# First layer of a four-layer trunk: 24 modulation chunks loaded in eleven groups, and their products placed elsewhere around the eight attention tiles

## The reference, cut to what matters

```python
def ada_mod(cond, w, b):
    m = jax.nn.silu(cond) @ w + b
    return [a[:, None, :] for a in jnp.split(m, 6, axis=-1)]
...
        sh1, sc1, gt1, sh2, sc2, gt2 = ada_mod(c, w_ada[li], b_ada[li])
        zsh1, zsc1, zgt1, zsh2, zsc2, zgt2 = ada_mod(cz, w_ada[li], b_ada[li])
        hx = modulate(x, norm_g[li, 0], sh1, sc1)
        hz = modulate(z, norm_g[li, 0], zsh1, zsc1)
        ...
            ox, oz = diff_attention(hx, hz, da_w_qkv[ia], da_w_o[ia], da_lambda[ia], da_subln[ia],
                                    lam_init, rows, cols, need_ctx)
        ...
        x = x + gt1 * ox
        x = x + gt2 * swiglu(modulate(x, norm_g[li, 1], sh2, sc2), ffn_in[li], ffn_out[li])
```

## Time and profile before

| what | value |
|---|---|
| median of 3 runs | 2442.58 us (2442.09, 2442.58, 2444.91) |
| time of the profiled execution | 2447.18 us |
| span of the profiled execution | 2445.4 us |
| PE busy | 2405.9 us (98%), 12338 matmuls |
| PE weight loads busy | 1983.0 us (81%) |
| VectorE busy | 1316.7 us (54%) |
| ScalarE busy | 1001.8 us (41%) |
| GpSimd busy | 1107.1 us (45%) |
| DMA | 340.62 MB, mean 139 GB/s |

### The profile page before, as it was taken

The page is one execution under the profiler, slowest core; times in us unless marked ns, Lnnn a source line. Parts: engine busy times, 40 slices in busy tenths (PEclk is TensorE's granted clock), DMA queues, the critical chain, the costliest instruction groups (busy, mean ns, idle before and its releaser), DMA issues.

```text
span 2445.4 us, 37489 instructions
## 1 busy us (share of the span) xinstructions
PE 2405.9 (98%) x12338; PEld 1983.0 (81%) x12338; DVE 1316.7 (54%) x2347; ACT 1001.8 (41%) x2023; POOL 1107.1 (45%) x839
## 2 busy tenths in 40 slices
PE   9999999999999999999999999999999999999998
PEld 4566788888888888888888887778888888778998
DVE  8997876647253334346664243655766524475321
ACT  3565442232243434433323234664323324466553
POOL 0432444445444344435445434223544543435896
PEclk9999999999999999999999999999999999999999
DMA  8362445556232222235555324222565532323654
GB/s 343 114 112 102 134 159 206 195 173 224 87 100 86 73 73 86 86 104 206 197 182 193 116 79 113 80 84 95 206 206 195 183 111 80 101 78 116 185 181 129
DMA packets 120869, 340.62 MB, mean 139 GB/s; under 512 B 35537, under 2 KB 41937, under 8 KB 120145
## 3 DMA queue, kind: packets, MB, share of 16 engines
q1 hardware_dynamic: 112754, 333.97, 41.8%
q10 hardware_dynamic: 8032, 5.52, 1.6%
HBM read 334.76 MB, written 4.69 MB: 139 GB/s over the span
## 4 chain that ended last, share of the span: by engine, by line
PE 50%; issue 31%; POOL 12%; DVE 4%; ACT 2%; DMA 1%; POOLq 0%; DVEq 0%; ACTq 0%; SPq 0%
PE low_banks L627 39%; POOL w_lo L620 12%; PE high_banks L627 10%; DVE h_lo L1964 1%; DVE tmp L1945 1%; DVE ssum_rstd L1801 0%; ACT w_hi L1276 0%; ACT e_x L1439 0%; DMA xT<-in_xT 0%; DVE rot L2139 0%; DMA ada_raw<-in_ada_w 0%; ACT lnm L1300 0%; DVE ssum_rstd L1933 0%; POOLq L619 0%; DMA w_raw<-in_weights 0%
## 5 line engine op out<-in xcount | busy, mean ns | idle before, releaser
L620 POOL TENSOR_TENSOR w_lo<-w_raw,w_hi 128x512 fp32r<-128x512 f32 x832 | 1106.7, 1357 | 1319.3 <-ACT w_hi L1276 1318.6
L627 PE MATMUL low_banks<-h_hi,w_hi 128*128 128x512 f32 (+2 forms) x1792 | 639.4, 357 | 5.0 <-POOL w_lo L620 1.8
L1276 ACT ACTIVATE w_hi<-w_raw 128x512 fp32r<-128x512 f32 x832 | 473.9, 624 | 395.4 <-PE low_banks L627 192.4
L627 PE MATMUL low_banks<-h_lo,w_hi 128*128 128x512 f32 (+2 forms) x1792 | 632.2, 353 | 0.0
L627 PE MATMUL low_banks<-h_hi,w_lo 128*128 128x512 f32 (+2 forms) x1792 | 630.6, 353 | 0.0
L1801 DVE SCALAR_TENSOR_TENSOR ssum_rstd<-ada_raw,high_banks 128x1024 f32<-128x1024 f32 x304 | 370.7, 1220 | 42.8 <-DMA ada_raw<-in_ada_w 33.9
L627 PEld LDWEIGHTS low_banks<-h_hi,w_hi 128*128 128x128 f32 x1792 | 337.9, 189 | 60.9 <-issue 4.8
L627 PEld LDWEIGHTS low_banks<-h_lo,w_hi 128*128 128x128 f32 x1792 | 338.1, 189 | 46.3 <-issue 1.0
L627 PEld LDWEIGHTS low_banks<-h_hi,w_lo 128*128 128x128 f32 x1792 | 337.1, 189 | 46.6
L1709 ACT ACTIVATE lnm<-low_banks 128x512 f32<-128x512 f32 x66 | 39.4, 597 | 378.2 <-PE low_banks L627 378.2
L2462 DVE TENSOR_TENSOR tmp<-low_banks,lnm 128x512 f32<-128x512 f32 x66 | 45.6, 692 | 211.3 <-ACT lnm L1709 207.6
(11 more groups left out here) (279 smaller groups left out, 3803.6 us busy)
## 6 DMA issues: line engine op xcount, KB each, us to landing
w_raw<-in_weights SPq DMA_DIRECT2D x424, 512.0 KB, 3.7
ada_raw<-in_ada_w SPq DMA_DIRECT2D x152, 512.0 KB, 3.8
ada_first<-in_ada_w SPq DMA_DIRECT2D x24, 512.0 KB, 9.1
v_all<-in_ada_w SPq DMA_DIRECT2D x10, 512.0 KB, 5.5
bias<-rpb_skew SPq DMA_DIRECT2D x64, 64.0 KB, 2.4
rpb_skew<-rpb_rows ACTq DMA_DIRECT2D x1, 3556.0 KB, 34.0
ada_rest<-in_ada_w SPq DMA_DIRECT2D x6, 512.0 KB, 14.0
cond_l<-in_cond SPq DMA_DIRECT2D x3, 1024.0 KB
```

What stands on the lines that cost most here:

```text
L620: nc.gpsimd.tensor_tensor(out=w_lo[:, r, part], in0=w_raw[:, r, part], in1=w_hi[:, r, part], op=ALU.subtract).then_inc(lo_ready, 1)
L627: return nc.tensor.matmul(dst, lhsT, rhs, start=start, stop=stop, **kw)
L1276: nc.scalar.activation(w_hi[:, r, part], w_raw[:, r, part], ACT.Copy).then_inc(hi_ready, 1)
```

## The change

It changes the tables, the place of the loads in SyncE's stream, and which chunks share one bias addition. The number of products (48) and of loads (24) stays.

```diff
-ADA_GROUPS = ((16, 0, (16, 17, 0, 4, 1, 5)), (22, 1, (2, 6, 3, 7)), (26, 0, (3,)), (27, 1, (7, 20, 21)),
-              (30, 0, (3, 7)), (32, 1, (20, 21, 22)), (35, 0, (20, 23)), (37, 1, (21, 22)), (39, 0, (20,)))
+ADA_GROUPS = ((16, 0, (16, 17, 0, 1, 5, 2)), (22, 1, (6, 3)), (24, 0, (7, 20)), (26, 1, (21, 3)), (28, 0, (7, 20)),
+              (30, 1, (21, 3)), (32, 0, (22, 20)), (34, 1, (21,)), (35, 0, (22, 23)), (37, 1, (20, 21)), (39, 0, (22,)))
 ADA_MIXER = 40
-ADA_VALUES = 4
-ADA_TILE = ((0, 1, 2), (1, 1, 1), (1, 1, 2), (1, 1, 2), (1, 1, 2), (1, 1, 2), (1, 1, 2), (1, 1, 2))
-ADA_TAIL = (1, 9)
+ADA_VALUES = 3
+ADA_TILE = ((0, 1, 1), (0, 0, 2), (1, 3, 0), (1, 3, 0), (1, 3, 0), (1, 3, 0), (1, 3, 1), (1, 3, 1))
+ADA_TAIL = (1, 10)
...
-            load_range(at, 24)
-
-            sp.wait_ge(ada_done, 25)
+            load_range(at, 22)
+
+            sp.wait_ge(plan[0].vst_ready, 2)
+            sp.wait_ge(ada_done, 22)
             ada_rest_load(2)
+            load_range(22, 24)
+
+            sp.wait_ge(plan[0].vst_ready, 4)
+            sp.wait_ge(ada_done, 24)
+            ada_rest_load(3)
+
+            sp.wait_ge(ada_done, 26)
+            ada_rest_load(4)
             load_range(24, 26)
...
+            sp.wait_ge(ada_done, 32)
+            ada_rest_load(7)
             load_range(30, plan[0].nf)
             at = plan[0].nf
 
-            sp.wait_ge(ada_done, 33)
             sp.wait_ge(plan[0].vst_ready, KT)
-            ada_rest_load(6)
+            sp.wait_ge(ada_done, 34)
+            ada_rest_load(8)
 
             sp.wait_ge(ada_done, 35)
-            ada_rest_load(7)
-
-            sp.wait_ge(ada_done, 36)
-            ada_rest_load(8)
+            ada_rest_load(9)
+
+            sp.wait_ge(ada_done, 37)
+            ada_rest_load(10)
...
-                    row = (a - a0) % LOOPED
+                    row = (a - ADA_FIRST) % LOOPED
...
-                        if row == LOOPED - 1 or a == a0 + len(slots) - 1:
-                            ada_sums(a - row, a - row, row + 1)
+                        if row == LOOPED - 1:
+                            ada_sums(a - row, a - row, LOOPED)
```

More of the change, by code:

```diff
@@ L511, in _ @@
             at = KT + RING
-            load_range(at, 24)
-            sp.wait_ge(ada_done, 25)
+            load_range(at, 22)
+            sp.wait_ge(plan[0].vst_ready, 2)
+            sp.wait_ge(ada_done, 22)
             ada_rest_load(2)
+            load_range(22, 24)
[4 more added lines that the diff above has]
+            ada_rest_load(4)
             load_range(24, 26)
-            sp.wait_ge(ada_done, 26)
-            sp.wait_ge(plan[0].vst_ready, 4)
-            ada_rest_load(3)
+            sp.wait_ge(ada_done, 28)
+            ada_rest_load(5)
             load_range(26, 28)
-            sp.wait_ge(ada_done, 28)
-            ada_rest_load(4)
+            sp.wait_ge(plan[0].vst_ready, 6)
+            sp.wait_ge(ada_done, 30)
+            ada_rest_load(6)
             load_range(28, 30)
-            sp.wait_ge(ada_done, 30)
-            sp.wait_ge(plan[0].vst_ready, 6)
-            ada_rest_load(5)
+            sp.wait_ge(ada_done, 32)
+            ada_rest_load(7)
             load_range(30, plan[0].nf)
             at = plan[0].nf
-            sp.wait_ge(ada_done, 33)
             sp.wait_ge(plan[0].vst_ready, KT)
-            ada_rest_load(6)
+            sp.wait_ge(ada_done, 34)
+            ada_rest_load(8)
             sp.wait_ge(ada_done, 35)
-            ada_rest_load(7)
-            sp.wait_ge(ada_done, 36)
-            ada_rest_load(8)
+            ada_rest_load(9)
+            sp.wait_ge(ada_done, 37)
+            ada_rest_load(10)
             def bias_load(L, t, slot, reused):
```

## The result

The changed kernel takes 2446.12 us (median of 22 runs, 2444.13 to 2450.25), the kernel before 2442.95 us (22 runs, 2440.93 to 2446.72). The ratio is 1.0014, with a 95% interval of 1.0008 to 1.002: some 3 us slower, and within the 0.2% that was called no difference. The forecast was 2444.9 us, which was 2.3 us over the median of three runs that stood before it (2442.58) and is 1.2 us under the measured one.

The account below looks back on a forecast made before the run. PE, busy 98% of the span, was taken to bound the kernel. Tile 7's scores 4.0 us earlier, 1.7 back in tail and projection: 2447.18 - 2.3 = 2444.9 us, range 2438.5 to 2451.5.

Parts of the forecast that it names:

- What bounds the kernel: Whole kernel: PE busy 98% of the span, so only its gaps and its clock can give time back.
- The fall in the other runs: Kernel before: the median run has the load wait but not the profiled execution's clock fall of 4.85 us.
- Up to T1: Until tile 1's scores start: fewer products ahead, gain 4.6 us, start at 108.4.
- T1 to T2: From tile 1's scores to tile 2's: loss 2.9 us, PE waits 2.35 us, tile 2 starts at 131.8.
- Five tiles: From tile 2's scores to tile 7's: 21.9 us each instead of 20.5, PE waiting 1.4 us for `kT` in each.
- Loads in the tiles: Tiles 2 to 7: loads cost nothing, read 26 us after issue; three landed within 8.1 us.
- Tail: Behind tile 7's scores and in the projection: VectorE waits 3.4 us for a load, PE 3.4; loss 1.7 us.
- The rule on GpSimd's ports: Products in tiles 2 to 5: VectorE contends with GpSimd; that rule alone gives back up to 7.6 us, sum 2437.3.
- A: Rival: clock falls in a new gap, 4.85 us each; one fall 2449.8 us (chance 0.3), two 2454.7 (0.08).
- the forecast's own list of what would show it wrong: Tiles of 20.5 us, granted clock under 1 behind the tail, or first maxima that set the weights' start.
- B: Rival in the tiles: key not late, tiles stay at 20.5 us, 7.7 us less, 2437.2 us; chance 0.12.
- D: Rival in SyncE's queue: the group's loads wait behind weight loads again; at most another 4.8 us, inside A.

Follow-up runs that it names:

- order: Kernel before with only the load group of chunks 27 to 29 issued ahead of weight units 24 and 25; 2437.20 us, 0.9975 to the kernel before.
- tail33: The change with the load group of chunks 35 and 36 released at 33 chunks done, not 34; 2444.03 us, 1.0002 to the kernel before.
- loads33: Kernel of loads with the group of chunks 35 and 36 released one chunk earlier; 2437.04 us, 0.9974 to the kernel before.
- half: The change with one of two moved products back behind the key in tiles 2 to 5, (1, 2, 1); 2440.26 us, 0.9989 to the kernel before.
- key4: The change with tiles 2 to 5 put back to (1, 1, 2), two products behind the key; 2440.32 us, 0.9987 to the kernel before.
- best1: The change with tail33's release, (1, 1, 2) in tiles 2 to 5 and (2, 1, 2) in tiles 6 and 7; 2438.18 us, 0.9981 to the kernel before.
- loads: The change's load groups, order and shared bias additions with the product places of the kernel before; 2438.75 us, 0.9983 to the kernel before.
- best2: best1 with one product more behind tile 0's key and one fewer in the tail; 2439.90 us, 0.9989 to the kernel before.

## Why the forecast was right

*What bounds the kernel.* Right. The load wait ahead of tile 4's weights was SyncE's order and nothing else. The forecast counted 5.1 us for it, and order gained 6.1, which leaves room for the clock's fall in part of the runs of before.

*The fall in the other runs.* The forecast took it that the median run of before has no fall. That is not borne out. Each run has its granted clock on record, as a mean over the whole program. On one chip it was 0.997 or less in 28 of 52 runs of the kernel before and in none of the 32 runs of order, tail33 and loads33, whose traces have no fall in these tiles. In the change it was 0.997 or less in 12 of 22. A mean does not say where the clock fell, and these traces have one at the end of the program too, so this shows that falls are common in both kernels and not how many there are in a run.

*Up to T1.* Forecast 108.4, measured 109.06 us. The gap for `a_z` did not close but kept 0.69 us, and the one for `kT` was 1.18 us where 0.9 was forecast. In five other profiles of the same program up to there T1 lies between 107.77 and 108.30.

*T1 to T2.* Forecast 131.8 with a wait of 2.35 us, measured 132.00 with 2.38. So close a hit has some luck in it: only one of the two products behind tile 1's key was slow (1.22 and 2.16 us), and VectorE reached the weights earlier than forecast, but then stood 0.70 us for ScalarE's exponential, which the chain did not have.

*Five tiles.* Right in size and in mechanism. The waits of 1.42 to 1.61 us stand against 1.4, the four tiles from T3 on take 22.10 us each ((244.01 - 155.61) / 4) against 21.93, and half shows by moving one product that this is the place. In tile 4 each step of the chain is where it was forecast: the last maximum at T + 6.89 us (6.88), the weights at T + 9.36 (9.38), the first product behind the query at T + 15.42 (15.44). T7 was 244.01 where 242.0 was forecast: 1.6 of the 2.0 us are the clock's fall behind T2 (23.61 us there, 22.00 in tail33, where it did not fall).

*Loads in the tiles.* Right in the change's trace: no wait for one. In loads33 there is one of 1.42 us, for a load issued more than 14 us before it was waited out, where the forecast had 8.1 us as the longest time to land.

*Tail.* Right in its steps. The wait for the load was 3.36 us (3.4), PE came back 30.82 us behind T7 (30.9 to 31.2) after a wait of 3.19 (3.4), and the wait for `xT` disappeared (0.3). tail33 shows that the release is the cause. The loss from T7 to the mean square's matmul was 2.6 us where 1.7 was forecast for tail and projection, and the clock's fall is 1.3 of it.

*The rule on GpSimd's ports.* What the Trainium skill says (GPSIMD Engine Reference, Specifications) is borne out in the instructions: the product behind tile 7's key took 2.08 us, those behind the queries 1.22. The 7.6 us that the forecast worked out for this rival did not come. VectorE's busy time did fall by 10.1 us, and key4 is faster by 6.6 us with its slow products than the change with its fast ones.

*Rivals.* A's mechanism came, its price was wrong. A granted clock under 1 behind the tail stood in the forecast's own list of what would show it wrong, and it was 0.50 there. The profile has two falls, which A priced at 4.85 us each. The one behind T2 cost 1.6 us. The one behind the last head cost about 1.3: from there to the mean square's matmul it is 22.61 us (297.44 - 274.83), and in tail33 22.48 with 1.15 us of waiting in it. So the two cost 2.9 us where 9.7 was the price, and the time stayed within 0.2%. That it did is luck in part: the forecast gave two falls a chance of 0.08 and left them out of its sum. The step that failed is the one that took the single fall of before, some 10 us long, for the price of any. B fell with the waits for `kT`, and key4 and half show their cause: the key is late. D did not come true.

The sum was 1.2 us too low against the medians (2446.12 - 2444.9). The two short falls, 2.9 us, are more than that in the profile. Part of the difference lies behind the projection, where the programs are the same and nothing was forecast: from the mean square's matmul to the end the change's profile has 2147.7 us and that of before 2148.5. How much the falls cost in the median run stays open, since only one execution of a kernel has a trace.

## What to carry to other kernels

Work that fills an engine beside another one has a right place: behind the result that the other engine waits for, in time that it has to wait out anyway. Two products there at up to 2.16 us cost PE nothing in key4's tiles 2 to 5, and the third product ahead of that result cost all of its 1.27 us. The reserve is not the same everywhere: in tile 7, where PE has less of its own work to do, two products behind the key made it wait. Count the small instructions that go along with a moved one (a bias addition of 1.1 us that best1's expectation had left out), and look for a load that is queued behind others before moving any work: one group of loads moved ahead of two weight loads gained 6.1 us, while all the new places together cost 7.6.

## What was not expected of the hardware

A gap does not have one price. The granted clock fell behind each of the six waits of PE of 2.71 us or more in these profiles (2.71, 2.92, 2.97, 3.18, 3.19, 3.30). Below that it depends on the execution. Behind one of 2.38 us it fell in the change, and behind one of 2.37 us it did not in tail33, a program that is the same up to there. Behind one of 1.93 us in tile 1 it fell in loads and not in loads33, again the same program up to there, and in best2 it fell behind one of 1.53 us. So a trace without a fall does not show that a kernel has none. The falls lasted from 3 us (276 to 279 in the change) to about 10 us in the kernel before. The price is about half of the length where PE is the slower engine, from 1.3 to 4.85 us, and it was nothing in loads, where PE would have waited anyway. What decides the length has no cause in these traces.

An addition on 128x8 numbers took 1.10 to 1.14 us beside GpSimd's work and 0.17 us away from it, six times as long, while the 128x1024 product went from 1.22 to as much as 2.1 or 2.3 us. Beside GpSimd, the short instruction is the dear one for its size.
